# Hybrid decoder layer on one core: x also laid out transposed, row scale applied behind the input projection

## The reference

```python
h = rms_norm(x, pre_mix_g[i])            # x * rsqrt(mean(x*x, -1) + EPS) * g
proj = h @ w_in[i]                       # 1024 x 3272
r_q, r_k, r_v, r_g, a_q, a_c, i_q, i_k, i_w = split_cols(proj)
c_kv = rms_norm(a_c, kv_norm_g[i])
q_lat = jnp.einsum('bshd,hdc->bshc', aq, w_uk[i]) * (DSA_HEAD_DIM ** -0.5)
ki = layer_norm(i_k, idx_k_norm_g[i], idx_k_norm_b[i])
rel = relu(einsum('bthd,bsd->bths', qi, ki)); iscore = einsum('bths,bth->bts', rel, wi)
_, sel = lax.top_k(iscore, 256)          # attention over the selected keys
```

## Time and profile before

| | |
|---|---|
| median of 3 runs | 1554.13 us (1552.19 to 1555.43) |
| the profiled execution | 1551.62 us |
| its span in the profile | 1549.8 us |
| TensorE busy | 1462.8 us (94%) |
| VectorE busy | 1090.0 us (70%) |
| ScalarE busy | 590.9 us |
| GpSimd busy | 245.6 us |

### The profile page before, as it was taken

The page is one execution under the profiler, slowest core; times in us unless marked ns, Lnnn a source line. Parts: engine busy times, 40 slices in busy tenths (PEclk is TensorE's granted clock), DMA queues, the critical chain, the costliest instruction groups (busy, mean ns, idle before and its releaser), DMA issues.

```text
span 1549.8 us, 19529 instructions
## 1 busy us (share of the span) xinstructions
PE 1462.8 (94%) x7060; PEld 1165.0 (75%) x7060; DVE 1090.0 (70%) x1615; ACT 590.9 (38%) x1130; POOL 245.6 (16%) x368
## 2 busy tenths in 40 slices
PE   5999999998779989999999999999999999999997
PEld 5887788886655566666678888888888788888886
DVE  4648969896678889994367777777777576657443
ACT  5344443215443444434443222222222365544211
POOL 5444456607700000000000000000000000000000
PEclk9999999999999999999999999999999999999999
DMA  6212223217110000001033454454445876763111
GB/s 198 74 52 77 67 87 110 98 67 289 48 55 28 28 28 28 14 15 55 15 95 111 138 175 169 164 180 166 163 163 199 289 260 235 237 218 122 56 55 41
DMA packets 134541, 180.82 MB, mean 117 GB/s; under 512 B 11824, under 2 KB 75056, under 8 KB 134448
## 3 DMA queue, kind: packets, MB, share of 16 engines
q1 hardware_dynamic: 118960, 144.99, 29.1%
q10 hardware_dynamic: 15488, 34.61, 5.8%
HBM read 126.09 MB, written 53.48 MB: 116 GB/s over the span
## 4 chain that ended last, share of the span: by engine, by line
PE 69%; DVE 11%; DVEq 6%; issue 5%; ACT 3%; POOL 3%; DMA 2%; SPq 1%; ACTq 0%; POOLq 0%
PE ps L662 19%; PE ps L664 19%; PE ps L663 19%; PE ps L888 5%; DVEq L1689 4%; DVE m L1686 3%; DVE lm L1778 2%; DVE sc L1675 2%; DVEq L1687 2%; PE ps L833 1%; DMA rb<-in_w_ffn_down 1%; PE ps L850 1%; PE ps L841 1%; ACT pt L1260 1%; PE ps L779 1%
## 5 line engine op out<-in xcount | busy, mean ns | idle before, releaser
L1686 DVE MAX8 m<-sc 128x8 f32<-128x384 f32 (+5 forms) x192 | 171.1, 891 | 13.1 <-issue 2.9
L1688 DVE MATCH_REPLACE8 sc<-m,sc 128x384 f32<-128x384 f32 (+5 forms) x192 | 168.2, 876 | 0.3 <-issue 0.3
L2193 POOL TENSOR_TENSOR smf<-smf,sml 128x1 f32<-128x1 f32 x16 | 9.1, 579 | 744.6 <-DVE smf L2100 630.2
L662 PE MATMUL ps<-wbh,xth 128*128 128x512 f32 (+1 forms) x320 | 119.9, 375 | 2.5 <-DVE xtl L1582 2.5
L662 PE MATMUL ps<-bh,ah 128*128 128x512 f32 x308 | 120.1, 390 | 0.1
L664 PE MATMUL ps<-bh,al 128*128 128x512 f32 x308 | 119.9, 389 | 0.0
L663 PE MATMUL ps<-bl,ah 128*128 128x512 f32 x308 | 119.8, 389 | 0.0
L663 PE MATMUL ps<-wbl,xth 128*128 128x512 f32 (+1 forms) x320 | 119.0, 372 | 0.0
L664 PE MATMUL ps<-wbh,xtl 128*128 128x512 f32 (+1 forms) x320 | 118.9, 372 | 0.0
L2044 DVE TENSOR_TENSOR al<-ra,ah 128x512 fp32r<-128x512 f32 x77 | 53.1, 690 | 79.4 <-ACT ah L1441 79.3
L1251 ACT ACTIVATE lm<-lm,sml 128x128 f32<-128x128 f32 (+7 forms) x64 | 49.6, 774 | 127.2 <-DVE sml L1778 126.6
(11 more groups left out here) (284 smaller groups left out, 3604.3 us busy)
## 6 DMA issues: line engine op xcount, KB each, us to landing
raw<-in_w_in SPq DMA_DIRECT2D x48, 256.0 KB, 3.1
wt<-in_w_ffn_down SPq DMA_DIRECT2D x44, 256.0 KB, 7.3
...
```

The lines of the kernel that those rows point to most:

```text
L662: pe.matmul(o, ah, wh, start=start, stop=False, skip_group_check=resumes)
L1686: v.max(M8[:, :], sc_b)
L1688: v.match_replace(sc_b, M8[:, :], sc_b, PICKED)
```

## The change

The host also hands over x transposed (`in_x_cols`) and the gain as a column. The kernel loads the transposed x in 8 model tiles (`XT[k]`), multiplies by the gain while it splits them (`x_hi(k)` and `x_lo(k)`, from SBUF now), and runs chunk 0 with the model dimension outermost (`first_units`), its 8 units in the 8 PSUM banks. The weights of chunk 0 are one tile (`WC0`, two DMAs, cast and split in two halves). The rows of x are loaded too, through three buffers (`XW`), for the squares alone. The row scale is applied behind the projection: to `AC` and to the scales of q and k (`SCL`) on VectorE in step 0, in ScalarE's evacuations, to the index weights, and to `AQ` on GpSimd with a copy of the row scales that goes through DRAM (`RSB`). The index queries stay unscaled: relu lets a positive factor of a row through, so the index weights are multiplied by it once more.

The diff, cut to what the text speaks of:

```diff
-    XN = [sb(f"xn{r}", [P, D], 148 + 4 * r if r < RT - 1 else 8) for r in range(RT)]
-    RAW = [sb(f"raw{i}", [P, 512], 140 + 2 * i if i < 4 else 184.5 + 2 * i) for i in range(8)]
+    XT = sb("xt", [P, KT, S], 44)
+    XW = [sb(f"xw{i}", [P, D], a) for i, a in enumerate((192.5, 196.5, 172))]
+    WC0 = sb("wc0", [P, KT, SMALL], 184)
+    RSB = sb("rsb", [P, S], 172)
+    RAW = [sb(f"raw{i}", [P, 512], 140 + 2 * i) for i in range(4)]
...
-    KEYS_AT = KT + 5
+    KEYS_AT = KT + 6
     LAST = NCH * KT
+    KEY_STEPS = {KT + 3: (0,), KT + 4: (1, 2), KT + 5: (3, 4), KT + 6: (5,), KT + 7: (6,)}
...
-        sp.dma_start(XN[0][:, :], x_t[:, 0, :]).then_inc(load_x[0], 16)
-        row_gain(GIN, pre_mix_g, "load_gin")
+        def load_xt(k):
+            sp.dma_start(XT[:, k, :], xt_dram[k * P:(k + 1) * P, :]).then_inc(load_x[k], 16)
+
+        def load_row(r):
+            sp.wait_ge(load_x[r], 16)
+            if r >= 3:
+                sp.wait_ge(s["a_sq"], r - 2)
+            sp.dma_start(XW[r % 3][:, :], x_t[:, r, :]).then_inc(load_x[r], 16)
+
+        sp.dma_start(GCOL[:, :], pre_mix_g).then_inc(s["load_gin"], 16)
+        load_xt(0)
+        wk = w_in[0].rearrange("(k p) c -> p k c", p=P)
+        sp.dma_start(WC0[:, :, 0:P], wk[:, :, C_AC:C_AC + P]).then_inc(s["load_gin"], 16)
+        sp.dma_start(WC0[:, :, P:SMALL], wk[:, :, C_IK:C_IK + HD + H]).then_inc(s["load_gin"], 16)
+        for k in range(1, KT):
+            load_xt(k)
         sp.dma_start(TAB[:, :], small_tab).then_inc(s["load_tab"], 16)
-        for n in range(4):
+        for n in range(KT, KT + 4):
             proj_weights(n)
-        sp.dma_start(XN[1][:, :], x_t[:, 1, :]).then_inc(load_x[1], 16)
-        for n in range(4, KT):
-            proj_weights(n)
-        for r in range(2, 5):
-            sp.dma_start(XN[r][:, :], x_t[:, r, :]).then_inc(load_x[r], 16)
         with nc.allow_non_contiguous_dma(reason="1024 positions, once"):
             sp.dma_start(POSI[:, :], positions[0].rearrange("(r p) -> p r", p=P)).then_inc(s["load_pos"], 16)
         sp.dma_start(INV[:, :], inv_freq).then_inc(s["load_pos"], 16)
...
+        load_row(0)
+        load_row(1)
+        for n in range(KT + 4, 2 * KT):
+            proj_weights(n)
+        load_row(2)
         row_gain(KVG, kv_norm_g, "load_const")
         row_gain(IKG, idx_k_norm_g, "load_const")
         row_gain(IKB, idx_k_norm_b, "load_const")
-
-        for g in range(-4, LAST):
+        for r in range(3, RT):
+            load_row(r)
+
+        for g in range(4, LAST):
             if g + 12 < LAST:
                 proj_weights(g + 12)
+            if g == 2 * KT:
+                sp.wait_ge(s["p_rs"], 1)
+                with nc.allow_non_contiguous_dma(reason="1024 row scales, once"):
+                    sp.dma_start(rs_dram[0].rearrange("(r p) -> p r", p=P), cols["rs0"]).then_inc(s["move_rs"], 16)
+                sp.wait_ge(s["move_rs"], 16)
+                sp.dma_start(RSB[:, :], rs_dram[0:1, :].to_broadcast([P, S])).then_inc(s["move_rs"], 16)
...
...
         def key_transposes():
 
             pe.wait_ge(s["v_kn"], 1)
-            pe.wait_ge(s["v_xl"], RT)
+            pe.wait_ge(s["a_ev"], KT)
+            pe.wait_ge(s["a_sq"], RT)
...
-        for r in range(RT + 2):
-            if r < RT:
-                row_transposes(r)
-            if r >= 2:
-                unit(r - 2)
+        def first_units():
+
+            for k in range(KT):
+                pe.wait_ge(s["v_xl"], k + 1)
+                if k % 4 == 0:
+                    pe.wait_ge(s["v_wlo"], k // 4 + 1)
+                for u in range(RT):
+                    rs = slice(u * P, (u + 1) * P)
+                    last = mm3(bank(u, SMALL), XTH[:, k, rs], XTL[:, k, rs], WBH[0][:, k, 0:SMALL], WBL[0][:, k, 0:SMALL],
+                               k == 0, k == KT - 1)
+                    if k == KT - 1:
+                        last.then_inc(s["t_unit"], 1)
+
+        first_units()
...
-            act.wait_ge(load_x[r], 16)
-            if r:
-                act.wait_ge(s["a_sq"], r)
-            sc.activation(pair(3), XN[r][:, :], ACT.Square, accum_out=cols["ss0"][:, r:r + 1]).then_inc(s["a_sq"], 1)
-
-        def x_hi(r):
-            act.wait_ge(s["t_xt"], r + 1)
-            sc.copy(XTH[:, :, r * P:(r + 1) * P], pair(1 + r % 2).rearrange("p (k c) -> p k c", k=KT))\
-              .then_inc(s["a_xh"], 1)
+            act.wait_ge(load_x[r], 32)
+            act.wait_ge(*((s["a_sq"], r) if r else (s["a_ev"], KT)))
+            sc.activation(pair(3), XW[r % 3][:, :], ACT.Square, accum_out=cols["ss0"][:, r:r + 1]).then_inc(s["a_sq"], 1)
+
+        def x_hi(k):
+            if k == 0:
+                act.wait_ge(s["load_gin"], 48)
+            act.wait_ge(load_x[k], 16)
+            sc.activation(XTH[:, k, :], XT[:, k, :], ACT.Copy, scale=GCOL[:, k:k + 1]).then_inc(s["a_xh"], 1)
+
+        def first_w_hi(half):
+            ks = slice(4 * half, 4 * half + 4)
+            sc.copy(WBH[0][:, ks, 0:SMALL], WC0[:, ks, :]).then_inc(s["a_wc"], 1)
...
-                    col = (QSC if j < 2 else KSC)[:, 2 * hp + j % 2:2 * hp + j % 2 + 1]
+                    c0 = H * (j // 2) + 2 * hp + j % 2
+                    col = SCL[:, r, c0:c0 + 1]
                     sc.activation(STG[n % 2][:, j * HD:(j + 1) * HD], o[:, j * HD:(j + 1) * HD], ACT.Copy, scale=col)
                 v01 = STG[n % 2][:, RV:RV + 384].rearrange("p (h c) -> p h c", h=2)[:, :, 0:HD]
-                sc.copy(v01, o[:, 2 * P:3 * P].rearrange("p (h c) -> p h c", h=2))
-                ins = sc.copy(STG[n % 2][:, RG_:RG_ + P], o[:, 3 * P:4 * P])
+                sc.activation(v01, o[:, 2 * P:3 * P].rearrange("p (h c) -> p h c", h=2), ACT.Copy, scale=row)
+                ins = sc.activation(STG[n % 2][:, RG_:RG_ + P], o[:, 3 * P:4 * P], ACT.Copy, scale=row)
...
...
-        act.wait_ge(s["v_ang"], 1)
-        sc.activation(SIN[:, :, :], ANR[:, :, :], ACT.Sin).then_inc(s["a_trig"], 1)
-        sc.activation(COS[:, :, :], ANK[:, :, :], ACT.Sin).then_inc(s["a_trig"], 1)
+        for k in range(KT):
+            x_hi(k)
+            if k < 2:
+                first_w_hi(k)
+            if k >= 4:
+                w_hi(KT + k - 4)
+        for n in range(KT + 4, 2 * KT):
+            w_hi(n)
+        for u in range(RT):
+            evacuate(u)
+        for r in range(4):
+            square(r)
         for g in range(KT, 2 * KT):
-            w_hi(g + KT)
             evacuate(g)
+            if g < KT + 2:
+                square(4 + 2 * (g - KT))
+                square(5 + 2 * (g - KT))
+            if g == KT + 3:
+                act.wait_ge(s["v_ang"], 1)
+                sc.activation(SIN[:, :, :], ANR[:, :, :], ACT.Sin).then_inc(s["a_trig"], 1)
+                sc.activation(COS[:, :, :], ANK[:, :, :], ACT.Sin).then_inc(s["a_trig"], 1)
+            if g >= KT + 4:
+                w_hi(2 * KT + 2 * (g - KT - 4))
+                w_hi(2 * KT + 2 * (g - KT - 4) + 1)
...
+        def x_lo(k):
+            if k == 0:
+                dve.wait_ge(s["load_gin"], 48)
+            dve.wait_ge(s["a_xh"], k + 1)
+            v.scalar_tensor_tensor(XTL[:, k, :], XT[:, k, :], GCOL[:, k:k + 1], XTH[:, k, :].bitcast(F32),
+                                   ALU.mult, ALU.subtract).then_inc(s["v_xl"], 1)
+
+        def first_w_lo(half):
+            dve.wait_ge(s["a_wc"], half + 1)
+            ks = slice(4 * half, 4 * half + 4)
+            v.tensor_tensor(WBL[0][:, ks, 0:SMALL], WC0[:, ks, :], WBH[0][:, ks, 0:SMALL].bitcast(F32), ALU.subtract)\
+             .then_inc(s["v_wlo"], 1)
+
+        def row_variance():
+            dve.wait_ge(s["a_sq"], RT)
+            v.tensor_scalar(cols["v0"], cols["ss0"], 1.0 / D, EPS, ALU.mult, ALU.add).then_inc(s["v_var"], 1)
...
+                dve.wait_ge(s["p_rs"], 1)
+                link(v.tensor_tensor(AC[:, :, :], AC[:, :, :], over(cols["rs0"], SMALL), ALU.mult))
+                v.tensor_tensor(SCL[:, :, :], TAB[:, 0:2 * H].unsqueeze(1).to_broadcast([P, RT, 2 * H]),
+                                over(cols["rs0"], 2 * H), ALU.mult)
...
-            key_norms(g - KT)
+            if g == KT + 2:
+                row_variance()
+            for step in KEY_STEPS.get(g, ()):
+                key_norms(step)
...
-            pool.wait_ge(s["v_var"], r + 1)
-            rsqrt(cols["rs0"][:, r:r + 1], cols["v0"][:, r:r + 1]).then_inc(s["p_rs"], 1)
-            if r < 4:
-                w_lo(2 * r)
-                w_lo(2 * r + 1)
-            else:
-                w_lo(r + 4)
+        for n in range(KT, 2 * KT):
+            w_lo(n)
+        pool.wait_ge(s["v_var"], 1)
+        rsqrt(cols["rs0"], cols["v0"]).then_inc(s["p_rs"], 1)
         link(g_.memset(TRI[:, :], 0.0))
         g_.affine_select(out=TRI[:, P:2 * P], in_=TRI[:, P:2 * P], compare_op=ALU.is_ge, fill=MASKED, base=0,
                          pattern=[[-1, P]], channel_multiplier=1).then_inc(s["p_tri"], 1)
-        for n in range(KT + 4, 3 * KT):
```

(22 more changed lines are left out.)

81 lines of the change are left out of this document (24 added, 57 removed).

## The result

The changed kernel takes 1567.76 us (median of 4 runs, 1565.75 to 1569.81), the kernel before 1553.16 (1552.04 to 1555.43): ratio 1.0088, interval 1.0076 to 1.0100. It is 14.6 us slower, where 6.0 were forecast. The profiled execution has a span of 1565.5 us against 1549.8.

The account below looks back on a forecast made before the run. It took the chain ending last, mostly TensorE, as the bound. 10.1 us won at chunk 0 less six losses gave -6.0: profiled 1551.6 to 1557.6, median 1554.1 to 1560.1 us, range 1555 to 1564.5.

Parts of the forecast that it names:

- the row scales' trip through DRAM: Store of the row scales to DRAM and broadcast back: counted as hidden, no cost in the sum.
- rival D: Row scales' store and broadcast hold up SyncE, staging tiles come late, TensorE stops 3 to 5 us, 1564; chance 0.12.
- chunk 0 sooner: Front of the kernel: chunk 0 ends at 43.6 against 53.74, 10.1 us won (8.4 to 12.2).
- loss 1: Row squares behind chunk 0 delay evacuations and so unit 12: 3.3 us (2.5 to 4.5).
- loss 2: Key transposes wait for the key norms from GpSimd and VectorE: 5.2 us, up to 6.5.
- loss 3: TensorE's clock runs lower behind the wait for the keys: 2.0 us (0 to 3.2).
- loss 4: First indexer scores wait for the low part of the keys, moved later on VectorE: 3.5 us (2.9 to 4.0).
- loss 5: TensorE's clock may run lower again behind the wait for the keys' low part: 1.2 us (0 to 2.5).
- loss 6: Queries' scale multiplies on GpSimd hold back clearing of the state tiles: 0.9 us (0.4 to 1.4).
- rival A: Small table does not queue, TensorE starts at 12.2, chunk 0 ends 7.3 us earlier: 1552.8; chance 0.07.
- Rival B: TensorE's clock stays up behind the waits for the keys and their low part: 1556.9; chance 0.13.

Follow-up runs that it names:

- one wait later: Changed kernel with the load back of the row scales, and SyncE's wait for their store, eight issue turns later: 1563.21 us, ratio 1.0050.
- trip early: Changed kernel with the row scales' store, wait and load all moved behind weight piece 23: 1562.16 us, ratio 1.0042.
- The squares early: Changed kernel with ScalarE's squares overwriting the row instead of PSUM, five ahead of chunk 0's evacuations: 1559.34 us, ratio 1.0030.
- the last kernel: Changed kernel with small table second, squares in place, row scales' store and load split, `kl` earlier, key norms' steps sooner: 1541.12 us, ratio 0.9923.

## Why the prediction was right and wrong

The sign and the places were right, the time was outside the range. The step that failed is the last line of the list of costs, "the row scales' trip through DRAM (hidden, below)", a term of the sum put at nothing. It is rival D, with a chance of 0.12. Its condition ("over some 6 us") was met almost twice over: 11.6 us for the store alone. The reason against it, that the next weight piece waits for GpSimd anyway, holds for only about half of the wait: GpSimd was done with its subtract at 111.3 us, and SyncE stood until 116.8. And it says nothing of the retention tile's store, which stood behind the same wait and for which ScalarE, and through it VectorE and TensorE, waited. In the trace of the changed kernel the trip makes 8.0 us, where D had 3 to 5. By the medians it is 4.9 (one wait later) and 5.9 (trip early), each uncertain by some 3 us, and by the table above 4.6 to 5.2 where the clock is less slow. So D's mechanism is shown and its price was about right for itself; what no term had is that the trip and the slow clock behind `kl` made each other dearer, as far as single traces can tell.

| term of the sum | forecast | measured |
|---|---|---|
| chunk 0 sooner | +10.1 | +12.9 |
| loss 1, row squares | 3.3 | 5.1 |
| loss 2, wait for the keys | 5.2 | 6.5 |
| loss 3, clock behind it | 2.0 | 2.5 (1.4 to 1.6 in four other traces) |
| loss 4, wait for `kl` | 3.5 | 3.3 |
| loss 5, clock behind it | 1.2 | 1.8 |
| row scales' trip | 0 | 8.0 (4.6 to 5.2 with less clock loss) |
| loss 6, scale on GpSimd | 0.9 | 1.0 |
| sum | -6.0 | -15.3 |

The measured column is the trace of the changed kernel. Loss 5 is what is left of 25.6 us from scores to MAX8 against 23.8 before, once the trip is out, so only loss 5 and the trip together, 9.8, are measured in this trace; with the trip first and the clock second the same 9.8 read 4.8 and 5.0. The trace has -15.5 at the state tiles, and the sum leaves 0.2 open.

Without the trip's 8.0 the column gives -7.3, near the -6.0 of the forecast. Part of that nearness is luck: chunk 0 came 2.8 us sooner than forecast, and losses 1, 2, 3, 5 and 6 together were 4.3 us dearer (loss 4 was 0.2 cheaper).

**Start.** The table queued, as the earlier trace rows had it; moved ahead, it freed TensorE at 11.99 (rival A's time without its mechanism). But the table came at 17.25, not 19.5: the transfers ran at 319 GB/s over the first 19.5 us, where I had taken the 259 of the earlier trace rows. Chunk 0 itself took 40.81 - 17.25 = 23.6 us for the 24.1 forecast.

**Loss 1.** The chain of squares and row loads was the right one, and undersized by 1.8 us in this trace. In six others with the same front the loss is 3.5 to 5.0, so the 3.3 forecast is at the low end. ScalarE's timeline of the changed kernel, the first two squares, and the fourth and the last with their waits:

```profile
41.43 1.03 ACT L1130 ACTIVATE ps<-xw 128x1024 f32<-128x1024 f32 x1
...
42.67 1.03 ACT L1130 ACTIVATE ps<-xw 128x1024 f32<-128x1024 f32 x1
...
46.26 1.03 ACT L1130 ACTIVATE ps<-xw 128x1024 f32<-128x1024 f32 x1 [1.20 <-DMA xw<-in_x]
...
55.16 1.03 ACT L1130 ACTIVATE ps<-xw 128x1024 f32<-128x1024 f32 x1 [2.13 <-DMA xw<-in_x]
```

A square takes 1.24 us from start to start, not 1.13, and the last begins 14.35 us behind unit 8's start, where I had 12.7. The slow clock behind the 2.34 us gap, which I had put inside the chain, also lies in this stretch; how much is each is not told apart. The squares early give 4.2 to 5.7 back.

**Loss 2.** The wait was 6.46 us, by chance the bound of 6.5 that the forecast gives for all four passes blocked. That bound was summed wrongly: with the forecast's own 6.3 us up to the passes, four blocked passes of 1.77 and TensorE there at 5.5, the wait would be 7.9, and 6.8 with three blocked. VectorE's and GpSimd's timelines of the changed kernel:

```profile
75.42 1.75 DVE L1692 TENSOR_TENSOR nxm<-nxm,sml 128x512 f32<-128x512 f32 x1 [1.16 <-POOL sml L2236]
77.20 1.64 DVE L1693 TENSOR_TENSOR nxm<-nxm,ikg 128x512 f32<-128x512 f32 x1
78.87 1.63 DVE L1695 TENSOR_TENSOR kn<-nxm,ikb 128x512 f32<-128x512 f32 x1
80.43 0.68 DVE L1696 TENSOR_TENSOR kn<-nxm,ikb 128x512 f32<-128x512 f32 x1
```

```profile
72.48 2.90 POOL L2236 TENSOR_TENSOR sml<-sml 128x16 f32<-128x16 f32 x1
75.36 4.60 POOL L2242 TENSOR_TENSOR wbl<-raw,wbh 128x512 fp32r<-128x512 f32 x3
```

Three passes beside GpSimd's three subtracts take 1.63 to 1.75 us, the one behind them 0.68. So three of the four were slowed, not two and not four. This agrees with the exclusive lock of the Trainium skill ("SBUF — State Buffer", Who interferes with whom). Whether the wait exists at all is a matter of where the steps stand: in the last kernel, with the steps sooner, it is gone.

**Clock.** Rival B is out for this kernel: the granted clock was at its lower level behind both waits, and filling them kept it at 1.00. The 3.3 us wait, which the forecast had left half open, did bring it here; in other traces the same wait was followed by 0.67, and once by 1.00, so the half-open term was the right way to write it.

**Page.** The Trainium skill, "DMA: Bandwidth & Descriptors", Rules for kernel authors, says that a transfer whose last dimension is not contiguous becomes one descriptor per element, and to rearrange it. The runs agree in kind: 1024 pieces of 4 bytes 11.6 us, 128 pieces of 32 bytes 2.6 us. The forecast had the pieces' size in rival D and did not weigh that sentence.
